# Differential heads scored in pairs on two sets of PSUM banks, in a two-block transformer kernel on one Trainium2 core

## What is computed

```python
proj = h @ w_in[i]                      # 1024 x 9216: qa, ka, va, qr, kr, vr, gr, gates
s = jnp.einsum('bqhcd,bkhcd->bhcqk', qb, k) * scale      # 8 heads, c = 2 halves of width 64
logits = jnp.where(dist >= 0, s - slopes * dist, -jnp.inf)
probs = jax.nn.softmax(logits, axis=-1)
a = probs[:, :, 0] - lam * probs[:, :, 1]
out = jnp.einsum('bhqk,bkhe->bqhe', a, v)                # v: (B, S, H, 128)
ya = rms_norm_2(out, g_diff_sub[i]) * (1.0 - lam_init)
```

## The kernel before

| count | engine | step, in the words of the text below |
|---|---|---|
| AT | TensorE | scores: `diff_scores`, 4 float32 matmuls on 64 rows each (two halves c) |
| AT + 1 | VectorE | maximum: `diff_max`, lines 1766 and 1769, adds the slope and finds the row maxima |
| AT + 2 | ScalarE | exponentials: `diff_exp`, line 1140 |
| AT + 3 | VectorE | combine: `diff_combine`, lines 1776 to 1785 |
| AT + 5 | TensorE, then ScalarE | turn: `diff_turn`, 3 transposes, and their copy to SBUF, `diff_copy`, line 1147 |
| AT + AV | TensorE | values: `diff_av`; AV = `DIFF_AV[h]`, 7 or 9 |
| AT + AV + 1, + 4, + 5, + 8 | VectorE, TensorE | clamp (line 1790); square sum (`diff_sum`, TensorE); parts (lines 1797, 1798); scale |

## Time and profile before

### The profile page before, as it was taken

The page is one execution under the profiler, slowest core; times in us unless marked ns, Lnnn a source line. Parts: engine busy times, 40 slices in busy tenths (PEclk is TensorE's granted clock), DMA queues, the critical chain, the costliest instruction groups (busy, mean ns, idle before and its releaser), DMA issues.

```text
span 906.6 us, 17567 instructions
## 1 busy us (share of the span) xinstructions
PE 895.1 (99%) x7068; PEld 861.3 (95%) x7068; DVE 677.2 (75%) x1196; ACT 476.2 (53%) x836; POOL 64.9 (7%) x137
## 2 busy tenths in 40 slices
PE   9999999999999999999999999999999999999996
PEld 7899999999999999997999989999999999999995
DVE  7776676778988878889789877786767666666666
ACT  5366355555655545566466644554335544444456
POOL 7023100120000000000000000000102000000000
PEclk9999999999999999999999999999999999999999
DMA  8554443645565656655644364656646666656651
GB/s 309 166 161 118 142 138 117 181 148 172 163 187 186 187 175 197 185 181 171 199 148 121 113 207 118 187 187 181 186 146 190 204 211 185 188 186 187 186 163 47
DMA packets 42544, 154.67 MB, mean 171 GB/s; under 512 B 4704, under 2 KB 5216, under 8 KB 42336
## 3 DMA queue, kind: packets, MB, share of 16 engines
q1 hardware_dynamic: 42320, 153.29, 54.8%
q10 hardware_dynamic: 144, 0.26, 0.1%
HBM read 152.48 MB, written 1.05 MB: 169 GB/s over the span
## 4 chain that ended last, share of the span: by engine, by line
PE 96%; DVE 2%; DMA 1%; ACT 1%; issue 0%; SPq 0%; ACTq 0%
PE bank L287 95%; DMA xc<-in_xT 1%; DVE wl L1362 0%; DVE va L1980 0%; PE bank L834 0%; DVE va L1983 0%; PE bank L468 0%; DVE work L1527 0%; ACT L1335 0%; ACT va L1311 0%; PE bank L681 0%; PE bank L469 0%; PE bank L471 0%; PE bank L682 0%; PE bank L683 0%
## 5 line engine op out<-in xcount | busy, mean ns | idle before, releaser
L1362 DVE TENSOR_TENSOR wl<-raw,wh 128x1024 fp32r<-128x1024 f32 x282 | 349.0, 1246 | 99.3 <-ACT wh L872 97.5
L872 ACT ACTIVATE wh<-raw 128x1024 fp32r<-128x1024 f32 x247 | 258.3, 1053 | 149.8 <-PE bank L287 142.6
L287 PE MATMUL bank<-a2h,wh 128*128 128x256 f32 x880 | 248.8, 284 | 0.0
L287 PE MATMUL bank<-a2h,wl 128*128 128x256 f32 x880 | 245.8, 280 | 0.0
L287 PE MATMUL bank<-a2l,wh 128*128 128x256 f32 x880 | 243.8, 280 | 0.0
L287 PE MATMUL bank<-a1h,wh 128*128 128x258 f32 (+1 forms) x736 | 208.2, 284 | 0.7 <-issue 0.6
L287 PE MATMUL bank<-a1h,wl 128*128 128x258 f32 (+1 forms) x736 | 206.0, 281 | 0.0
L287 PE MATMUL bank<-a1l,wh 128*128 128x258 f32 (+1 forms) x736 | 203.5, 282 | 0.0
L287 PEld LDWEIGHTS bank<-a2h,wh 128*128 128x128 f32 x880 | 165.7, 188 | 3.0 <-issue 2.7
L287 PEld LDWEIGHTS bank<-a2h,wl 128*128 128x128 f32 x880 | 165.6, 188 | 0.0
L287 PEld LDWEIGHTS bank<-a2l,wh 128*128 128x128 f32 x880 | 164.5, 188 | 0.2
(11 more groups left out here) (267 smaller groups left out, 1086.4 us busy)
## 6 DMA issues: line engine op xcount, KB each, us to landing
raw<-in_wts SPq DMA_DIRECT2D x284, 512.0 KB, 3.7
csb<-in_cst SPq DMA_DIRECT2D x1, 1364.0 KB, 9.6
xc<-in_xT SPq DMA_DIRECT2D x1, 816.0 KB, 7.7
va<-in_gfin SPq DMA_DIRECT2D x1, 512.0 KB, 4.7
out<-va SPq DMA_DIRECT2D x1, 512.0 KB, 2.6
xc<-in_xT SPq DMA_DIRECT2D x1, 276.0 KB, 4.0
va<-in_pT SPq DMA_DIRECT2D x1, 256.0 KB, 4.0
out<-va ACTq DMA_DIRECT2D x1, 256.0 KB, 2.6
```

The lines of the kernel that those rows point to most:

```text
L287: return e.matmul(o, lhsT, rhs, start=start, stop=stop, skip_group_check=True)
L872: e.activation(wh[:, i % NHL, :], raw[:, i % NRAW, :], ACT.Copy).then_inc(s_hi, 1)
L1362: e.tensor_tensor(lo, src, hi.bitcast(F32), ALU.subtract).then_inc(s_lo, 1)
```

## The change

The scores of heads h and h + 1 (h even) are issued together, at the count `DIFF_AT[h]` of the even head. Each of the two has its own pair of banks, (3, 4) or (5, 2), and transposes into the first bank of its own pair. This takes bank 2 from the projection tiles: tiles 0 to 23 use banks 0 and 1 in turn, and tile t waits for EV t - 2. The steps of all heads are at new counts. On ScalarE and VectorE `DIFF_AT[h]` still sets the place of each head's own steps, the odd head's maximum among them. The copy of head 7 goes back to its regular place, and head 6's clamp and square as well.

```diff
-DIFF_AT = [6, 10, 14, 18, 24, 28, 34, 38]
+DIFF_AT = [10, 12, 18, 21, 28, 31, 38, 41]
 DIFF_AV = [7, 7, 9, 9, 9, 9, 9, 9]
...
-        B_S2, B_T2, B_O2 = (3, 4), 5, (6, 7)
-        RET_SUM = lambda h: bank[B_S2[0] if h % 2 else B_T2][:, 0:S]
-        VR_BANK = ((0, 1), (2, 5))
+        B_S2, B_O2 = ((3, 4), (5, 2)), (6, 7)
+        B_T2 = lambda h: B_S2[h % 2][0]
+        B_RS = (3, 4)
+        RET_SUM = lambda h: bank[3 if h % 2 else 5][:, 0:S]
+        VR_BANK = ((2, 5), (0, 1))
+        PROJ2_BANK = lambda t: t % 2 if t < 24 else (2, 0, 1)[(t - 28) % 3]
...
+                elif h == 1:
+                    e.wait_ge(s_ln, 5)
                 else:
-                    e.wait_ge(s_dm, 5 * (h - 1) + 4)
+                    e.wait_ge(s_dm, 5 * (h - 2) + 4)
+                    e.wait_ge(s_dc, h - 1)
...
             def diff_turn(h):
                 ee = work[:, 4 * (h % 2), 0:384]
-                tb_ = bank[B_T2]
+                tb_ = bank[B_T2(h)]
                 e.wait_ge(s_dn, 6 * h + 6)
-                if h:
-                    e.wait_ge(s_dc, h)
...
-                    if j == 0:
+                    if j == 0 and h % 2 == 0:
                         diff_scores(h)
+                        diff_scores(h + 1)
...
             def proj2(t, i, p):
-                if t == 2:
-                    e.wait_ge(s_ln, 5)
-                elif t >= 3:
+                if 2 <= t < 24:
+                    e.wait_ge(*ev2(t - 2))
+                elif t >= 28:
                     e.wait_ge(*ev2(t - 3))
...
                 if r == 0:
+                    e.wait_ge(s_dc, 8)
+                else:
                     e.wait_ge(*ev2(22))
-                else:
                     e.wait_ge(*ev2(23))
-                    e.wait_ge(s_dc, 8)
...
-                    elif j == 5 and h < 7:
+                    elif j == 5:
                         diff_copy(h)
-                    elif a == (0 if h == 6 else 2):
+                    elif a == 2:
                         diff_square(h)
...
-                if t == 21:
-
-                    hi_to(i + 5)
-                    diff_copy(7)
                 pump2(p + 1)
...
-                    elif a == (0 if h == 6 else 1):
+                    elif a == 1:
                         diff_clamp(h)
```

More of the change, by code:

```diff
@@ L669, in diff_scores @@
                     k = qk[64 * c:64 * c + 64, 8 + h, 0:S]
-                    s = bank[B_S2[c]]
+                    s = bank[B_S2[h % 2][c]]
                     mm(s[:, 0:128], q[:, 0:128], k[:, 0:128], True, False)
@@ L702, in ret_scores @@
             def ret_scores(h):
-                s = bank[B_S2[h % 2]]
+                s = bank[B_RS[h % 2]]
                 e.wait_ge(*ev2(23))
                 if h < 2:
-                    e.wait_ge(s_dm, 5 * 7 + 4)
+                    e.wait_ge(s_dc, 8)
                 else:
@@ L755, in proj2 @@
             def proj2(t, i, p):
-                if t == 2:
-                    e.wait_ge(s_ln, 5)
-                elif t >= 3:
+                if 2 <= t < 24:
+                    e.wait_ge(*ev2(t - 2))
+                elif t >= 28:
                     e.wait_ge(*ev2(t - 3))
-                tile(i, bank[t % 3][:, 0:S], A2[0], A2[1], range(KT), mid=lambda: pump2(p)).then_inc(s_blk, 1)
+                tile(i, bank[PROJ2_BANK(t)][:, 0:S], A2[0], A2[1], range(KT), mid=lambda: pump2(p)).then_inc(s_blk, 1)
                 pump2(p + 1)
@@ L1146, in diff_copy @@
                     e.wait_ge(s_do, h - 1)
-                e.activation(work[:, 4 * (h % 2) + 3, 0:384], bank[B_T2][:, 0:384], ACT.Copy).then_inc(s_dc, 1)
+                e.activation(work[:, 4 * (h % 2) + 3, 0:384], bank[B_T2(h)][:, 0:384], ACT.Copy).then_inc(s_dc, 1)
             def diff_square(h):
@@ L1765, in diff_max @@
                     for j, (a, b) in enumerate(DK):
-                        e.tensor_tensor_reduce(work[:, 4 * par + c, a:b], bank[B_S2[c]][:, a:b], bias[:, a:b], 1.0, NEG,
+                        e.tensor_tensor_reduce(work[:, 4 * par + c, a:b], bank[B_S2[par][c]][:, a:b], bias[:, a:b], 1.0, NEG,
                                                ALU.add, ALU.max, mx[:, 2 * c + j:2 * c + j + 1]).then_inc(s_dm, 1)
@@ L1820, in ret_decay @@
                     e.wait_ge(s_dt, 8)
-                e.tensor_tensor(work[:, 4 * par, 0:384], bank[B_S2[par]][:, 0:384], decay[:, h, :], ALU.mult).then_inc(s_rp, 1)
+                e.tensor_tensor(work[:, 4 * par, 0:384], bank[B_RS[par]][:, 0:384], decay[:, h, :], ALU.mult).then_inc(s_rp, 1)
             def ret_copy(h):
@@ L1894, in proj2 @@
                     pump2(p + 1)
-                o = bank[t % 3][:, 0:S]
+                o = bank[PROJ2_BANK(t)][:, 0:S]
                 e.wait_ge(s_blk, i + 1)
```

## The result

| | median (range), us | runs |
|---|---|---|
| before | 907.92 (907.72 to 908.29) | 4 |
| changed | 921.29 (919.86 to 921.56) | 4 |

The ratio is 1.0139 (95% interval 1.0127 to 1.0151): 12.6 us slower by it (the medians differ by 13.4), where 7.7 were forecast. The profiled execution of the changed kernel is its fastest, 919.86 us with a span of 918.6.

What follows compares the result with a forecast made beforehand. TensorE was taken to bound the kernel, with VectorE 88% busy in the stretch: 907.83 - 1.64 - 0.27 + 9.38 + 0.2 = 915.5, median 915.6 us. Own range 914.0 to 917.0; with rivals 912.6 to 918.6.

Steps and rivals of the forecast that it cites:

- the mechanism of the waits: VectorE runs two maxima and two combines, with ScalarE's exponentials between, ahead of each odd head's turn, so TensorE waits there.
- signs of being wrong: Forecast wrong if waits at turns sum to under 7 us, or new ones at tile starts to over 1 us.
- granted clock stays 1.00: Expected in the new profile: TensorE's granted clock stays at its upper level, 2.4 GHz.
- The waits at the odd turns: TensorE waits for VectorE's combines before turns 1, 3, 5, 7: 1.52, 2.13, 3.64, 2.09, together +9.38 us.
- rival 2: TensorE's clock falls to 1.2 GHz in the 3.64 us wait, slowing one or two tiles: 918 to 920; chance 0.06.
- The price of a fall: At 1.2 GHz, 256 columns take 0.213 us, not 0.119: 2.3 us for each tile until the clock is back.
- A shared passage: Scores pay 0.41 us per passage into 64 rows and back; eight groups becoming four save four: -1.64 us.
- The wait at turn 3: Heads 2, 3: combine 3 starts 8.25 us after EV 10, turn possible at 10.25, TensorE there at 8.12: 2.13 us.
- Smaller waits: Slow LO steps on VectorE, up to 1.63 us against a 1.22 median, falling on a chain: 0.2 us taken.
- The two banks and the banks of the turns: Two banks in place of three cost nothing; worst case tile 23, at most 0.1 us, inside turn 7's wait.
- -0.27: Existing TensorE waits before two turns for VectorE's combine, which the change removes: 0.27 us.

Runs made afterwards that it cites:

- filled: Changed kernel plus 9, 15 and 8 matmuls of ones, read by nobody, ahead of the turns of heads 3, 5 and 7: 916.62 us, ratio 1.0097.
- retimed_b: Changed kernel, paired scores, each step at new counts of its own, last values ahead of the retention values: 908.61 us, ratio 1.0001.
- retimed: Changed kernel, same pairs and banks, counts of all steps chosen anew so that no turn should wait: 909.27 us, ratio 1.0014.
- two_banks: Kernel before the change with only tiles 0 to 23 put into two banks in turn: 908.77 us, ratio 1.0004.
- old_counts: Changed kernel with the old counts and each head's scores in a group of their own: 908.24 us, ratio 1.0002.
- scores_apart: Changed kernel with each head's scores at their own count again, eight groups, all else as changed: 915.73 us.
- retimed_apart: `retimed` with the odd head's scores one count later, in a group of their own: 909.36 us, ratio 1.0012.
- retimed_c: As `retimed_b` with other counts, maxima back to back, head 1's combine directly behind head 0's: 907.81 us, ratio 0.9992.

## Why the prediction was wrong, step by step

Direction and the mechanism of the waits were right; what the waits do to the clock was left out of the sum, and the time was 921.3 where 918.6 was the end of the range. Of the prediction's own signs of being wrong, none came at the waits (10.0 us where under 7 would have been wrong, one tile start of 0.1 to 0.2 us where over 1 would have been); its "granted clock stays 1.00" did not hold.

- **The waits at the odd turns: right.** Forecast 1.52, 2.13, 3.64 and 2.09, together 9.38. Measured from start to start, over what the same matmuls take where nothing waits: heads 0 and 1 1.61 (0.23 at turn 0, 1.38 at values 0 and turn 1), then 2.54, 3.74 and 2.08, together 9.97; the 3.74 is from `filled`, where the clock stays up. The mechanism of the longest is in the trace as forecast, VectorE idle ahead of LO 17, which waits for a split that stands behind the exponentials, and the combine of head 5 behind it. This is the timeline of ScalarE and VectorE ahead of turn 5:

```profile
501.41 0.49 ACT L1145 ACTIVATE work<-work,smallh 128x256 f32<-128x256 f32 x1
...
501.91 1.04 ACT L877 ACTIVATE wh<-raw 128x1024 fp32r<-128x1024 f32 x1
...
502.98 1.23 DVE L1363 TENSOR_TENSOR wl<-raw,wh 128x1024 fp32r<-128x1024 f32 x1 [2.55 <-ACT wh L877]
...
504.12 0.17 DVE L1777 RECIPROCAL smallh<-smallh 128x4 f32<-128x4 f32 x1
...
505.57 0.48 DVE L1786 SCALAR_TENSOR_TENSOR work<-work,smallh 128x256 f32<-128x256 f32 x1
```

- **The step that failed: rival 2, "The wait of 3.64 us is the only candidate", with a chance of 0.06.** The clock fell behind it and behind the wait of 2.0 at turn 7, 3.41 us each time, and that cost 2.7 us in the profiled execution. A fall should have been part of the forecast once it had a wait of 3.64: before the change the trace showed no wait inside the stretch, so nothing in it spoke for the clock's staying up. Its one long idle stretch behind matmuls is at the end, where the last matmul ends at 898.8 and the clock falls at 903.1, 4.3 us later (columns as in the earlier trace rows):

```profile
898.90:903.10 4.20, 0.00 (x0) 0.00 (x0) 3.03 (x10) 3.04 (x7) 0.37 (x1) 1.00 0.30 125
903.10:906.60 3.50, 0.00 (x0) 0.00 (x0) 0.50 (x1) 0.47 (x1) 0.00 (x0) 0.50 0.40 152
```

  One such time, from a single trace, does not say that a wait of 3.64 is safe: the other traces have 2.1 to 5.2 at the same place. The chance of 0.06 had no row behind it, and the waits of 2.09 and 2.13 were not asked about at all. The price of a fall was put at 2.3 us for each tile; a whole fall costs 1.1 to 1.6.
- **A shared passage: mis-sized.** 0.31 us, not 0.41; -1.24 in place of -1.64, 0.4 us. The prediction's own row had the right size: if two heads in one group pay 0.50 and two groups 0.82, a shared passage saves 0.32, and four of them 1.28. The sum took the whole 0.41 instead.
- **The wait at turn 3: 0.4 more than forecast**, and not by a slow LO. Combine 3 starts 8.21 us behind EV 10 (8.25 forecast), but one of its instructions takes 0.77 us where it took 0.35 in combine 2, and GpSimd runs an addition for an earlier head at that time. The timeline of VectorE and GpSimd:

```profile
474.10 0.35 DVE L1786 SCALAR_TENSOR_TENSOR work<-work,smallh 128x128 f32<-128x128 f32 x1
...
481.17 0.17 DVE L1777 RECIPROCAL smallh<-smallh 128x4 f32<-128x4 f32 x1
...
481.85 0.73 POOL L2078 TENSOR_TENSOR qk<-tmpb,qk 128x256 f32<-128x256 f32 x1 [3.47 <-ACT qk L1163]
481.96 0.77 DVE L1786 SCALAR_TENSOR_TENSOR work<-work,smallh 128x128 f32<-128x128 f32 x1
```

  That the one slows the other is argued from the overlap; no run tested it. The fourteen traces bear it out: on this kind of instruction (both its sizes) in the stretch, 214 without GpSimd at work beside it took 0.35 to 0.49 us, and of the 10 with such an addition beside it 8 took 0.77 to 0.93, one of them in `retimed_b` and one in `retimed`, at another head.
- **Smaller waits: 0.2 forecast (for slow LOs), some 0.3 measured**, in pieces of 0.2 and less. One of them is that of tile 23 for its bank, whose first matmul starts right behind EV 21:

```profile
524.61 0.41 DVE L1902 SCALAR_TENSOR_TENSOR va<-bank,rb 128x256 f32<-128x256 f32 x1
525.08 0.39 PE L290 MATMUL bank<-a2h,wh 128*128 128x256 f32 x1
```
- **The two banks and the banks of the turns: right**, 0.1 us at the old counts (`two_banks`, `old_counts`), and 0.1 to 0.2 at tile 23 where the forecast had at most 0.1, ahead of the wait for turn 7, which it shortens.
- **Sum again, without the clock:** -1.24 - 0.27 + 9.97 + 0.3 = 8.8 us, and the lag of `filled`, where the clock stays up, is 8.90 at 545.5. With 2.7 for the two falls it is 11.5, and the lag of the changed kernel is 11.64. Its profiled execution lost 0.67 more far behind the change (last section) and was 0.37 ahead where the stretch begins: 907.83 + 11.64 + 0.67 - 0.37 = 919.8, measured 919.86. That the median is 1.4 higher is not explained.
- **What the forecast did not ask: whether pairing helps at all.** It booked the shared passages as a gain beside the waits. `scores_apart` showed that, while the odd turns wait, the odd scores ahead of the maxima lengthen three of these waits by their own length. With waits nearly gone (`retimed`, `retimed_apart`) the pairs are worth 0.6 us in the traces and nothing that the medians can tell. The loss is the work of the counts, with the pairs on top: the banks cost 0.1, the counts without pairs have a ratio of 1.0089 (`scores_apart`), with pairs 1.0139, and pairs with other counts 0.9992 to 1.0038.

## What to carry to other kernels

When a table of times moves two dependent chains closer together, work the chain out on the engine between the two steps of the critical one, here VectorE, before asking what the critical engine saves: 0.3 us saved in each of four places was worth nothing against waits of 2 to 4 us. Work of the critical engine that stands inside such a wait is free, and moving it ahead of the chain cost nearly its full length here, 0.92 to 1.05 us of 1.06. And where a wait of some microseconds is forecast on TensorE, where the trace has none, put the fall of its clock into the sum, or fill the wait with products that nobody reads: here that gave back 3.8 us of 12.6 by the ratios, of which 2.7 can be traced to the clock.

## What the runs showed of the hardware that was not expected

- **The clock falls after waits as short as 2.0 us, and not after each.** Every stretch at the lower level inside the kernel was 3.41 us long, though TensorE had work for all of it but 0.2 us at most, and a fall cost 1.1 to 1.6 us. They began between 0.2 us before and 0.7 us after the start of a turn 5 that had waited 3.67 us, 1.3 us after one that had waited 2.6 and 1.2 and 1.3 us after a turn 7 that had waited 2.0. The Trainium skill, "TensorE: Matmul & The Clock Gate", Why this matters for your kernels, advises against idle gaps between bursts of matmuls. The traces agree for six of these ten waits; behind the other four the granted clock stayed 1.00.
- **Matmuls of the same code have different paces at the upper level.** Some 45 us behind the last tile of the change all kernels run the same twenty weight blocks (566 to 624 us in the trace of before), with TensorE always busy at clock 1.00. The window 571 to 611 of before, of `retimed_c` and of `two_banks`:

```profile
571.00:611.00 40.00, 40.00 (x344) 40.00 (x343) 31.74 (x51) 23.27 (x40) 0.00 (x0) 1.00 0.63 194
```

```profile
571.00:611.00 40.00, 40.00 (x339) 40.00 (x338) 31.28 (x52) 23.28 (x40) 0.00 (x0) 1.00 0.67 198
```

```profile
571.00:611.00 40.00, 40.00 (x336) 40.00 (x335) 30.81 (x51) 22.66 (x39) 0.00 (x0) 1.00 0.65 188
```

There are 344, 339 and 336 matmuls in 40 us: a block takes 2.82, 2.85 or 2.88 us, where the blocks behind them take 2.84 in every trace. The lag grows here by 0, 0.65 or 1.3 us, in steps of 0.03 or 0.06 for each block, and hardly in front of it or behind: the difference between the columns 556.4 and the end in the table above. No edit of the text goes with it (`two_banks` has 1.3, `old_counts` 0; seven traces have 0, six 0.65). With one trace for each kernel it is not shown whether it belongs to the kernel or changes between executions; what sets it is open. It is as large as what the pairs could gain, and if it changes between executions it is part of why those of one kernel lie 1 to 3 us apart. Of two traces, then, compare places right behind the change before comparing ends.
- **Two heads' scores, back to back in one group of 64-row matmuls, lose 0.1 us at their border** (1.81 against 2 x 0.65 + 0.41 = 1.71), where the two halves of the second head start 0.11 us apart and those of the first 0.01.
